# The opening of a two-block transformer kernel: norms moved behind the products, x loaded in halves, sums of squares on TensorE

## What is computed

```
h = rms_norm(x, mix_norm_g)                  # x * rsqrt(mean(x*x) + eps) * g
proj = h @ w_in                              # pool, q_down, kv_down, k_rope, xq, gate_logits
y_mem = cross_attention(xq, rms_norm(mem, mem_norm_g), w_mem_kv)
cos, sin = rope_tables(positions)            # angle = position * inv_freq
gates = sigmoid(gate_logits + gate_b)
merged = sum over branches of gates * (y_branch @ w_branch)
x = x + merged @ w_out ; then a mixture of experts, then two blocks of another kind
```

## Time and profile before

| | |
|---|---|
| median of 3 runs | 3946.32 us (3942.91 to 3949.37) |
| profiled execution | 3946.55 us, span 3944.5 us |
| TensorE (PE) busy | 3657.5 us, 93% |
| VectorE busy | 1809.8 us, 46% |
| GpSimd busy | 1322.1 us, 34% |
| ScalarE busy | 1058.2 us, 27% |
| mean granted TensorE clock | 0.970 of full |

### The profile page before, as it was taken

The page is one execution under the profiler, slowest core; times in us unless marked ns, Lnnn a source line. Parts: engine busy times, 40 slices in busy tenths (PEclk is TensorE's granted clock), DMA queues, the critical chain, the costliest instruction groups (busy, mean ns, idle before and its releaser), DMA issues.

```text
span 3944.5 us, 70993 instructions
## 1 busy us (share of the span) xinstructions
PE 3657.5 (93%) x27376; PEld 3268.3 (83%) x27376; DVE 1809.8 (46%) x2845; ACT 1058.2 (27%) x1609; POOL 1322.1 (34%) x568
## 2 busy tenths in 40 slices
PE   3898998799789999999899999999999999899998
PEld 2776776533289998989789999999999888799998
DVE  6456636211253357343547424642474334564246
ACT  2323222011122223333432212221224333432122
POOL 2242343133234442313124434343432222144443
PEclk9999998699899999999999999999999999999999
DMA  2221232699512221222112223222321222022232
GB/s 85 69 86 47 71 94 71 265 375 357 192 61 94 86 96 55 79 68 80 38 54 86 94 85 98 77 94 84 98 83 44 81 71 70 25 89 86 90 91 91
DMA packets 104082, 390.76 MB, mean 99 GB/s; under 512 B 22992, under 2 KB 23120, under 8 KB 91472
## 3 DMA queue, kind: packets, MB, share of 16 engines
q1 hardware_dynamic: 86176, 369.46, 28.0%
q10 hardware_dynamic: 3888, 10.14, 0.8%
q0 software_dynamic: 13824, 8.44, 0.7%
HBM read 438.28 MB, written 16.78 MB: 115 GB/s over the span
## 4 chain that ended last, share of the span: by engine, by line
PE 78%; issue 11%; DVE 5%; POOL 2%; DVEq 1%; DMA 1%; ACT 1%; POOLq 0%; SPq 0%; ACTq 0%
PE ps L595 63%; PE ps L907 4%; PE ps L714 2%; PE ps L917 2%; PE ps L701 2%; POOL w_lo L2423 2%; PE ps L727 2%; DVEq L1497 1%; DVE weigh L1694 1%; DMA e_w_lo<-in_wexp,cs 1%; PE ps L899 1%; PE ps L627 0%; PE ps L862 0%; PE ps L731 0%; DVE kb L1594 0%
## 5 line engine op out<-in xcount | busy, mean ns | idle before, releaser
L2423 POOL TENSOR_TENSOR w_lo<-raw,w_hi 128x1024 fp32r<-128x1024 f32 (+1 forms) x466 | 1224.7, 2628 | 2309.0 <-ACT w_hi L1134 2308.9
L595 PE MATMUL ps<-h_hi,w_hi 128*128 128x264 f32 (+1 forms) x4656 | 1022.3, 296 | 39.6 <-ACT qb L1151 8.2
L1134 ACT ACTIVATE w_hi<-raw 128x1024 fp32r<-128x1024 f32 (+1 forms) x466 | 514.7, 1105 | 2028.0 <-PE ps L595 1975.4
L595 PE MATMUL ps<-h_lo,w_hi 128*128 128x264 f32 (+1 forms) x4656 | 1014.8, 294 | 0.0
L595 PE MATMUL ps<-h_hi,w_lo 128*128 128x264 f32 (+1 forms) x4656 | 1013.3, 294 | 0.0
L595 PEld LDWEIGHTS ps<-h_hi,w_hi 128*128 128x128 f32 x4656 | 741.6, 190 | 64.8 <-DVE h_lo L2176 15.8
L595 PEld LDWEIGHTS ps<-h_lo,w_hi 128*128 128x128 f32 x4656 | 738.5, 190 | 13.6 <-issue 0.5
L595 PEld LDWEIGHTS ps<-h_hi,w_lo 128*128 128x128 f32 x4656 | 737.8, 190 | 13.9
L595 PE MATMUL ps<-hid_hi,w_hi 128*128 128x264 f32 (+2 forms) x2376 | 544.3, 299 | 22.4 <-DVE qb L1578 10.6
L595 PE MATMUL ps<-hid_hi,w_lo 128*128 128x264 f32 (+2 forms) x2376 | 541.2, 298 | 0.0
L595 PE MATMUL ps<-hid_lo,w_hi 128*128 128x264 f32 (+2 forms) x2376 | 539.7, 297 | 0.0
(11 more groups left out here) (331 smaller groups left out, 3643.5 us busy)
## 6 DMA issues: line engine op xcount, KB each, us to landing
raw<-in_w SPq DMA_DIRECT2D x402, 512.0 KB, 3.5
raw<-in_w SPq DMA_DIRECT2D x64, 704.0 KB, 4.0
e_hid_hi<-in_wexp SPq DMA_DIRECT2D x24, 1024.0 KB, 5.6
e_hid_lo<-in_wexp SPq DMA_DIRECT2D x24, 1024.0 KB, 10.5
merged<-in_wexp SPq DMA_DIRECT2D x16, 1024.0 KB, 6.2
e_h_lo<-in_wexp SPq DMA_DIRECT2D x16, 1024.0 KB
e_h_hi<-in_wexp SPq DMA_DIRECT2D x16, 1024.0 KB, 7.3
aux<-in_tab ACTq DMA_DIRECT2D x16, 408.0 KB, 3.7
```

The costliest lines, as they stand in the source:

```text
L595: ins = pe.matmul(ps[:, 2 * b + bank, 0:m], u, v[:, at:at + m], start=(k == 0 and i == 0), stop=(k == last and i == 2))
L1134: act.activation(w_hi[:, slot, 0:width * P], raw[:, slot, 0:width * P], ACT.Copy).then_inc(hi_done, 1)
L2423: pool.tensor_tensor(w_lo[:, slot, cols], raw[:, slot, cols], w_hi[:, slot, cols].bitcast(F32), ALU.subtract).then_inc(lo_done, 1)
```

## The change

The inputs get semaphores of their own: x comes in two halves of four chunks (`x_in`), mem has `mem_in`, the gains and resident tables have `const_in`, and meta, positions and the mask `rest_in`. Positions are now issued by ScalarE. The parts of x and mem are made from `x * gain` with no root in it, x first, and ScalarE squares each chunk just ahead of its rounding. TensorE takes the 16 chunks of squares itself, with accumulating products by the matrix of ones. The inverse roots `x_root` and `mem_root` are computed behind that, and every result on x or mem in the block is multiplied by its inverse root as it leaves PSUM (`scaled_x`, `scaled_mem`) instead of being copied. The gate's bias moves into the Sigmoid. `merged` is cleared before the first parts. The angles take 11 instructions (twelve with the drain behind them) instead of 20.

```diff
...
-            norm_sum(MEM)
-            norm_sum(SEQ)
-            x_normed = (h_ready, T.next("h", DC))
+            for first, n, of in ((0, SEQ, x_squares), (DC, MEM, mem_squares)):
+                b = take()
+                for c in range(DC):
+                    pe.wait_ge(squares, first + c + 1)
+                    ins = pe.matmul(ps[:, 2 * b, 0:n], ones, of[:, n * c:n * (c + 1)], start=c == 0, stop=c == DC - 1)
+                ins.then_inc(acc_full[b], 1)
+            x_written, mem_parts = (h_ready, 0), (h_ready, DC)
...
+                            act.activation(s_sb[:, d % 2, 0:n], t32[:, d % 2, 0:n], ACT.Sigmoid,
+                                           bias=p1[:, bass.ds(i * 4 + col, 1)]).then_inc(gate_ready, 1)
...
-            split(0, 0)
+            act.dma_start(cs[:, 0, 0:SEQ].bitcast(I32), positions.to_broadcast([P, SEQ])).then_inc(rest_in, 16)
+            act.dma_start(masks[:, 0:SEQ], tables[:, causal:causal + SEQ]).then_inc(rest_in, 16)
+            act.wait_ge(const_in, 2 * 16)
+            for c in range(DC):
+                if c % 4 == 0:
+                    act.wait_ge(x_in[c // 4], 16)
+                act.activation(x_squares[:, SEQ * c:SEQ * (c + 1)], X[:, c, META:L], ACT.Square).then_inc(squares, 1)
+                act.wait_ge(normed_chunk, T.next("normed"))
+                act.activation(h_hi[:, c, 0:SEQ], t32[:, 2 * (c % 2), 0:SEQ], ACT.Copy).then_inc(normed_hi, 1)
+            act.wait_ge(mem_in, 16)
+            for c in range(DC):
+                act.activation(mem_squares[:, MEM * c:MEM * (c + 1)], mem_raw[:, MEM * c:MEM * (c + 1)], ACT.Square).then_inc(squares, 1)
+                if c == 1:
+                    split(0, 0)
             split(1, 0)
-            act.wait_ge(const_in, CONST_INS)
-            norm(MEM, DC, lambda c: mem_raw[:, MEM * c:MEM * (c + 1)])
-            norm(SEQ, DC, lambda c: X[:, c, META:L], to_h=True)
+            for c in range(DC):
+                act.wait_ge(normed_chunk, T.next("normed"))
+                act.activation(hid4_hi[:, MEM * c:MEM * (c + 1)], t32[:, 2 * (c % 2), 0:MEM], ACT.Copy).then_inc(normed_hi, 1)
+            for out, n in ((x_root, SEQ), (mem_root, MEM)):
+                b, k = full()
+                root(b, out, n, D)
...
+            def scaled_x(out, use=None):
+                b, k = use or full()
+                ve.tensor_tensor(out, acc(b, SEQ), x_root, ALU.mult).then_inc(acc_free[b], 1)
...
-            ve.memset(aux[:, 1, :], 0.0)
-            ve.wait_ge(const_in, CONST_INS)
+            ve.memset(aux[:, 1, SEQ:], 0.0)
+            ve.memset(merged[:, :, :], 0.0)
+            ve.wait_ge(const_in, 2 * 16)
...
+                for c in range(DC):
+                    if c in in_:
+                        ve.wait_ge(in_[c], 16)
+                    ve.tensor_scalar(t32[:, 2 * (c % 2), 0:n], src(c), p_of(gain, c), None, ALU.mult).then_inc(normed_chunk, 1)
+                    uses.append(T.next("normed"))
+                    if c:
+                        lo_part(c - 1)
+                        settle()
+                lo_part(DC - 1)
...
+            for root in (x_root, mem_root):
+                b, k = skip()
+                ve.wait_ge(acc_free[b], k + 1)
+                ve.reciprocal(root, root)
+            ve.wait_ge(rest_in, REST_INS)
...
-                    copy(qb[:, hd, 0:SEQ], SEQ)
-                    copy(kb[:, hd, 0:MEM], MEM)
+                    scaled_x(qb[:, hd, 0:SEQ])
+                    scaled_mem(kb[:, hd, 0:MEM])
...
-            sp.dma_start(X[:, :, META:L], x).then_inc(const_in, 16)
-            sp.dma_start(X[:, :, 0:META], meta).then_inc(const_in, 16)
-            sp.dma_start(flat(qb[:, :, :])[:, 0:DC * MEM], mem).then_inc(const_in, 16)
+            for half in range(2):
+                chunks = slice(DC // 2 * half, DC // 2 * (half + 1))
+                sp.dma_start(X[:, chunks, META:L], x[:, chunks, :]).then_inc(x_in[half], 16)
+            sp.dma_start(mem_raw[:, 0:DC * MEM], mem).then_inc(mem_in, 16)
+            sp.dma_start(X[:, :, 0:META], meta).then_inc(rest_in, 16)
```

More of the change, by code:

```diff
@@ L62 @@
 PI_IN = 3.1415925
-CONST_INS = 7 * 16
+REST_INS = 3 * 16
 ACC_T, ACC_O = 2, 3
@@ L316, in build @@
         const_in = sem("const_in")
+        x_in = [sem(f"x_in{i}") for i in range(2)]
+        mem_in = sem("mem_in")
+        rest_in = sem("rest_in")
         layer_in = sem("layer_in")
@@ L1239, in paired_attention, with merge, gate @@
                 T.next("p_turned", 2 * len(pairs))
-            def merge(n, deep):
-                def gate(d):
-                    b, k = last_of_panel()
-                    act.wait_ge(gate_used, T.next("gate"))
-                    act.wait_ge(acc_free[b], k + 1)
-                    act.activation(s_sb[:, d % 2, 0:n], t32[:, d % 2, 0:n], ACT.Sigmoid).then_inc(gate_ready, 1)
-                with T.loop(act, 2, **(MERGE8 if deep else MERGE4)):
+            def merge(n, deep, branch=None):
+                with T.loop(act, 2, **(MERGE8 if deep else MERGE4)) as i:
+                    def gate(d):
+                        b, k = last_of_panel()
+                        act.wait_ge(gate_used, T.next("gate"))
+                        act.wait_ge(acc_free[b], k + 1)
+                        if branch is None:
+                            act.activation(s_sb[:, d % 2, 0:n], t32[:, d % 2, 0:n], ACT.Sigmoid).then_inc(gate_ready, 1)
+                        else:
+                            col = G1["gate_b"] + DC * branch + d
+                            act.activation(s_sb[:, d % 2, 0:n], t32[:, d % 2, 0:n], ACT.Sigmoid,
+                                           bias=p1[:, bass.ds(i * 4 + col, 1)]).then_inc(gate_ready, 1)
                     for two in range(2):
@@ L1251, in merge @@
                             for one in range(2):
-                                gate(one)
+                                gate(2 * two + one)
                                 last_of_panel()
@@ L1542, in norm_of_summed @@
                 norm_tail(n, src, gain, DC, write)
-            def norm(n, src, gain, write, chunks=DC):
-                ve.drain().then_inc(src_ready, 1)
-                base = T.now("squares")
-                T.next("squares", chunks)
-                for c in range(1, chunks):
-                    if c > 1:
-                        settle()
-                    ve.wait_ge(squares, base + (c + 1))
-                    ins = ve.tensor_tensor(merged[:, 0, 0:n], merged[:, 0, 0:n], merged[:, c, 0:n], ALU.add)
-                ins.then_inc(sums_ready, 1)
-                norm_tail(n, src, gain, chunks, write)
             def sum_squares(total, tmp, parts):
@@ L1762, in paired_attention, with merge @@
                 T.next("p_spread", len(closed))
-            def merge(n, deep, bias, branch, into):
+            def merge(n, deep, first, into):
                 with T.loop(ve, 2, **(MERGE8 if deep else MERGE4)) as i:
@@ L2061, in _ @@
             for c in range(2):
-                copy(qb[:, c, 0:SEQ], SEQ)
+                scaled_x(qb[:, c, 0:SEQ])
             settle()
@@ L2065, in _ @@
             b_kv, k_kv = skip()
-            copy(qb[:, 2, 0:SEQ], SEQ)
+            scaled_x(qb[:, 2, 0:SEQ])
             settle()
@@ L2097, in _ @@
                 u, a, c = qb[:, g, 0:SEQ], t32[:, 0, 0:SEQ], t32[:, 1, 0:SEQ]
-                copy(u, SEQ)
+                scaled_x(u)
                 settle()
```

93 lines of the change are left out of this document (46 added, 47 removed).

## The result

| | before | changed |
|---|---|---|
| median | 3945.27 us (4 runs, 3942.91 to 3949.37) | 3906.12 us (4 runs, 3904.34 to 3910.14) |
| ratio, 95% interval | | 0.9906 [0.9893, 0.9918] |
| profiled execution, span | 3946.55 us, 3944.5 us | 3905.6 us, 3903.9 us |
| granted TensorE clock | 0.970 | 0.972 |

The change gains 39.2 us by the medians and 37 us by the ratio, with an interval of 32 to 42 us. The forecast of 3904 us is 2 us away, yet the opening did not run as I had written it. TensorE first, then the windows, cut where I had put the first and the fifth product (22 and 48 us) and where the rest begins (60 us).

What follows compares the result with a forecast made beforehand. TensorE's chain of products sets the end, behind an opening chained over three engines. Fifth product 40.0 us earlier plus 2.3 us to the value transposes is 42.3 us, off 3946.3 us: 3904 us, range 3899 to 3911.

Steps and rivals of the forecast that it cites:

- rival A: Opening: TensorE stays at 1.2 GHz through the sums of squares, total 3918 to 3925 us; chance 0.12.
- Start, parts of x, squares of mem: Opening: memsets done at 7.6 us, x's fifteen activations from 8.15 to near 17.5 us, mem squares and two panels until 22.2 us.
- Rival B: Opening: ScalarE's table loads or DMA issues hold the first squares, up to 4.5 us, 3907 to 3910 us; within forecast's 0.82.
- TensorE sums the squares: Opening: the ones-products start at 7.2 us, speed up to 2.4 GHz and catch up with squares every 1.25 us.
- so the first product starts at about 22 us: Opening: first product follows the sum over mem, at about 22 us instead of 53.27, and ends at 29 us.
- Parts of mem, Roots: Opening: parts of mem done at 30.1 us with one block charged; root of x at 31.6, both reciprocals at 36.7 us.
- TensorE meanwhile: Opening: third product waits for panel 2 until 36.8 us and ends at 41.3 us; the fourth ends at 47.0 us.
- Angles: VectorE, opening: eleven instructions take 6.6 us plus two 2.0 us blocks, ending at 47.3 us; first evacuation at 48.0 us.
- Fifth product and the end: End of opening: fifth product at 48.1 instead of 88.12 us, worth 40.0 us; sixth ends at 54 us, another 2.3 us.
- Behind the opening: After the value transposes: 46 evacuations become products at 0.691 us like copies, bias goes into the Sigmoid; counted as 0.
- rival C: Slower than before: evacuations blocked beside GpSimd's subtractions, up to 1.8 us each, 3987 us with all on the path; chance 0.02.
- The rule weighed: VectorE and GpSimd lock a shared port, also for two SBUF inputs; four blocks rather than three make the sum 40.3 us.

Runs made afterwards that it cites:

- changed_again: The changed kernel itself, run once more as the zero for the delay runs; median 3912.36 us, ratio 0.9914.
- sums_in_2_3: Changed kernel with the two sums of squares in PSUM accumulators 2 and 3 instead of 0 and 1; median 3898.45 us, 3903.77 us when repeated.
- roots_early: Changed kernel with ScalarE's two roots ahead of its eight roundings of mem, sums left in accumulators 0 and 1; median 3905.52 us, ratio 0.9900.
- old_angles: Changed kernel with the twenty angle instructions of the kernel before; median 3909.72 us, ratio 0.9910.
- sums_on_vector: Changed kernel, but VectorE adds up the squares and TensorE makes one product with ones for each of x and mem; median 3925.96 us, ratio 0.9952.
- delay_8: Changed kernel with two more memsets of merged, each with a drain, ahead of VectorE's first part of x; median 3914.98 us, ratio 0.9924.
- angles_late: Changed kernel with sums in accumulators 2 and 3, roots ahead of mem's roundings, and angles behind the loop of two; median 3903.78 us, ratio 0.9905.

## Why the prediction was right, and where it was not

**Right in mechanism but for one step, and right in total with some luck.** The sum was 42.3 us up to the start of the rest; measured 36.5 us, 5.8 us less. The rest, counted at 0, gave 4 us in the profiled run, which is within its scatter and which nothing in the change explains. How near the total came is therefore luck: the same kernel in changed_again had a median of 3912.36 us, a gain of 34 us by the ratio. One of the signs that I had named for a wrong prediction did come, a first product after 28 us, though not for the reason given there (A).

In the list, "forecast" marks my number beside the measured one.

- *Start, parts of x, squares of mem.* The first rounding of x began at 8.63 us (forecast 8.15), the last ended at 17.15 us (forecast 17.5); the roundings of mem start at 21.39 us (forecast 22.2). The first square was late: I had TensorE's stream begin at 7.2 us, and the square began at 8.01. The first half of x was there at 6.23 us, as forecast, but the tables only at 8.01 us, and VectorE's memsets ended at 8.3 instead of 7.6 us. A pace of 1.13 us a chunk made up for it. Rival B is out: ScalarE's four DMA issues ended at 3.05 us. The halves, which I priced only as a risk, are what makes 8 us possible: in one piece x costs 5.7 us at the first square.
- *TensorE sums the squares.* A pass takes 1.06 us until 13.2 us, the slow level, and 0.59 us from 13.75 us on. At the slow level one product, two passes started 0.85 us apart, takes 1.7 us, and the squares come every 1.1 us: the engine had no gap until it had sped up. The eight products of x take 9.42 us and those of mem 3.88 us, less than 0.5 us each. They end at 21.9 us as forecast, so the engine sped up within the sums and rival A is out. In the Trainium skill, "TensorE: Matmul & The Clock Gate", section "What's actually happening", the slow level is the default that only activity leaves; the trace agrees, with 1.06 and then 0.59 us a pass in a stream without a gap.
- **The failed step: "so the first product starts at about 22 us".** It started at 31.05 us, at the slow level until 34 us. I had worked out operands and weights, and not where the product's output goes. `take()` starts again at accumulator 0 in the loop, which held the sum over x until ScalarE's root; and ScalarE takes the roots only behind the roundings of mem. In my own sum the root of x ended at 31.6 us, under the words "no longer ahead of the products, only ahead of the copies": those words are wrong by the accumulator, and sums_in_2_3 (21.71 us) and roots_early (23.54 us) show it by undoing it in two ways.
- *Parts of mem, Roots.* One block (2.36 us at 21.83), done at 29.5 us (forecast 30.1); the root of x starts at 30.32, the reciprocals end at 36.0 us (forecast 36.7).
- *TensorE meanwhile.* The third product, put at 36.8 us, came at 43.25: ScalarE's next panel needs the first product's end. The fourth ended at 53.3 instead of 47.0 us.
- *Angles.* They took 6.5 us (forecast 6.6) and two blocks of 2.1 and 2.2 us, and the first evacuation ended at 48.2 us (forecast 48.0). But the step lost most of its effect, since the fourth product was now last. The 2 us of before's angles that old_angles still shows, against 7.4 without the late first product, are the measure.
- *Fifth product and the end.* 53.27 us and not 48.1; the sixth waited 0.73 us for panel 5 and the rest began at 60.03 us instead of 54: 5.8 us less than summed.
- *Behind the opening.* The 24 gates' products have a mean of 691 ns (before, with the bias, 750 ns) and the Sigmoid with its bias 710 ns (619). No evacuation from PSUM was blocked, beside the same panels of GpSimd: rival C is out. The two rows are these, of VectorE's and ScalarE's groups in the changed kernel:

```profile
L1601 DVE TENSOR_TENSOR t<-ps,aux 128x512 f32<-128x512 f32 x24 | 16.5, 691 | 76.0 <-PE ps L603 75.3 <-issue 0.5
```

```profile
L1263 ACT ACTIVATE s_all<-t,p 128x512 f32<-128x512 f32 x24 | 17.0, 710 | 0.5 <-DVE t L1601 0.5
```

- *The rule weighed.* The Trainium skill, "SBUF — State Buffer", section "SBUF: two separate sides", has VectorE blocked also with two SBUF inputs. The trace agrees: the subtraction at 21.83 us took 2.36 us instead of 0.42, in GpSimd's panel of 21.57 to 23.91 us. In roots_early the three SCALAR_TENSOR_TENSORs of the angles took 4.41 us instead of 2.23, beside a panel. There were three blocks up to the fifth product, as charged.

**What stays open.** Why sums_on_vector loses more behind its opening than its start explains: 10 to 12 us against the changed kernel's first runs, 6 to 8 against changed_again. In its profiled run the distance to the changed kernel, matched activation by activation, grows in small steps, from 5 us at 200 us to 23 us at 3500 us. The mean granted clocks of the two profiled runs, 0.969 and 0.972, give by an estimate some 25 us more at the slow level, worth 12 us; but changed_again, at 0.970, had a rest as short as the changed kernel's (3844 us), so the clock alone is not shown to be the cause. A drift of this size is not peculiar to this run: sums_in_2_3 goes, matched in the same way, from 10 us ahead at 500 us to 2 us behind at the end. delay_8, 1.7 us later still at the start of the rest, was 2.6 us longer than changed_again, which speaks against lateness as the cause; the intervals of the two ratios overlap slightly. For angles_late nothing has to be placed: its profiled run keeps its lead, with a rest of 3845 us, and the missing 7 us of its median are about the size of its interval.

## What to carry to other kernels

A product can start when its operands, its weights and its output buffer are there: write down all three for the first use of each buffer behind a moved step, above all where a loop starts the buffer count again. An edit off the bound is worth what the slack leaves of it (the angles: 2.4 or 7.4 us), so price it again after each wait that is removed. sums_in_2_3 is the version to take: two changed buffer numbers in each of three lists, and medians 7.7 and 8.6 us under the changed kernel's, the second of them beside it on one chip. angles_late starts the rest another 2 us earlier, but its median does not show that it is better.
